# Routed-expert gate matrices built token by token from fp32r one-hots, one token behind each chunk of a projection unit

## What is computed

```python
q = (xb @ w_q).reshape(p, PEER_HEADS, 2, PEER_DK_HALF)
sc = jnp.einsum('phcd,hcnd->phcn', q, sub_keys)
top_s, top_i = lax.top_k(sc, PEER_TOPK)
...
best_s, best_pos = lax.top_k(cand_s, PEER_TOPK)
idx = jnp.take_along_axis(cand_i, best_pos, axis=-1)
g = jax.nn.softmax(best_s, axis=-1)
act = jax.nn.gelu(jnp.einsum('phkd,pd->phk', expert_u[idx], xb), approximate=False)
coef = g * act
return jnp.einsum('phk,phkd->pd', coef, expert_v[idx])
```

## Time and profile before

| | us |
|---|---|
| median of 3 runs (1960.28 to 1960.56) | 1960.36 |
| the profiled execution | 1959.54 |
| its span, first to last instruction | 1957.7 |
| mean granted clock, share of full | 0.965 |
| PE busy in the span | 1835.4 (94%) |
| DVE busy | 1579.7 (81%) |
| POOL busy | 1041.4 (53%) |
| ACT busy | 701.5 (36%) |

### The profile page before, as it was taken

One profiled execution on the slowest core, in us unless ns is written; L12 is line 12 of the kernel. 1 busy time (PEld: TensorE's weight loads), 2 busy tenths in 40 slices (PEclk: granted clock), 3 DMA queues, 4 the chain that ended last, 5 costly groups with the idle time before them and its releaser, 6 DMA issues.

```text
span 1957.7 us, 29019 instructions
## 1 busy us (share of the span) xinstructions
PE 1835.4 (94%) x10357; PEld 1593.5 (81%) x10357; DVE 1579.7 (81%) x2585; ACT 701.5 (36%) x1122; POOL 1041.4 (53%) x648
## 2 busy tenths in 40 slices
PE   8899889999999999999999999999999998988885
PEld 7677767999999899999978887888887676766664
DVE  6877777869898898888499999999997868757656
ACT  2333333433333444444433333333334333224441
POOL 1333235588888655555666676767774542344001
PEclk7898889999999999999999999999999998999988
DMA  7641242588999789899999999999995131200011
GB/s 297 222 167 54 65 162 84 181 303 308 314 310 316 249 295 309 300 307 306 320 351 358 354 354 351 354 352 353 364 353 175 55 96 54 76 22 3 2 59 50
DMA packets 159918, 440.49 MB, mean 225 GB/s; under 512 B 13648, under 2 KB 62928, under 8 KB 156752
## 3 DMA queue, kind: packets, MB, share of 16 engines
q1 hardware_dynamic: 64400, 254.71, 37.9%
q0 software_dynamic: 36864, 134.23, 18.2%
q10 hardware_dynamic: 58560, 50.34, 7.8%
HBM read 386.80 MB, written 52.43 MB: 224 GB/s over the span
## 4 chain that ended last, share of the span: by engine, by line
PE 71%; DVE 16%; issue 4%; POOL 4%; ACT 2%; DMA 2%; ACTq 0%; DVEq 0%; PEldq 0%; POOLq 0%
PE PS L947 32%; PE PS L1232 24%; PE PS L1195 4%; POOL w_lo L840 3%; DVE arena L2101 2%; PE PS L967 2%; ACT w_hi L1446 1%; DMA raw<-in_expert_v 1%; PE PS L1258 1%; DVE arena L1836 1%; PE PS L1267 1%; DMA arena<-in_expert_u_rows,arena 1%; POOL arena L888 1%; DVE arena L2128 1%; DVE arena L2125 1%
## 5 line engine op out<-in xcount | busy, mean ns | idle before, releaser
L840 POOL TENSOR_TENSOR w_lo<-raw,w_hi 128x1024 fp32r<-128x1024 f32 x299 | 719.2, 2406 | 786.1 <-ACT w_hi L1446 785.2
L1446 ACT ACTIVATE w_hi<-raw 128x1024 fp32r<-128x1024 f32 x332 | 351.7, 1060 | 982.8 <-PE PS L947 628.7
L947 PE MATMUL PS<-act_hi,w_hi 128*128 128x384 f32 (+1 forms) x1584 | 582.3, 368 | 25.3 <-POOL w_lo L840 19.0
L947 PE MATMUL PS<-act_hi,w_lo 128*128 128x384 f32 (+1 forms) x1584 | 567.4, 358 | 0.0
L947 PE MATMUL PS<-act_lo,w_hi 128*128 128x384 f32 (+1 forms) x1584 | 567.0, 358 | 0.0
L947 PEld LDWEIGHTS PS<-act_hi,w_hi 128*128 128x128 f32 x1584 | 302.2, 191 | 67.4 <-POOL w_lo L840 16.3
L947 PEld LDWEIGHTS PS<-act_hi,w_lo 128*128 128x128 f32 x1584 | 302.5, 191 | 22.8 <-issue 1.4
L947 PEld LDWEIGHTS PS<-act_lo,w_hi 128*128 128x128 f32 x1584 | 301.7, 190 | 23.6
L1232 PE MATMUL PS<-w_hi,act_hi 128*128 128x512 f32 x768 | 300.2, 391 | 7.0 <-ACT arena L1598 2.9
L1232 PE MATMUL PS<-w_lo,act_hi 128*128 128x512 f32 x768 | 299.3, 390 | 0.0
L1232 PE MATMUL PS<-w_hi,act_lo 128*128 128x512 f32 x768 | 299.2, 390 | 0.0
(11 more groups left out here) (347 smaller groups left out, 2001.5 us busy)
## 6 DMA issues: line engine op xcount, KB each, us to landing
raw<-in_expert_u SPq DMA_DIRECT2D x128, 512.0 KB, 5.3
raw<-in_expert_v SPq DMA_DIRECT2D x128, 512.0 KB, 6.0
raw<-in_w_in SPq DMA_DIRECT2D x52, 512.0 KB, 3.7
arena<-in_w_ada SPq DMA_DIRECT2D x24, 1024.0 KB, 7.2
gel_d<-arena ACTq DMA_DIRECT2D x64, 384.0 KB
gates_d<-arena ACTq DMA_DIRECT2D x12, 2048.0 KB, 15.9
arena<-gates_d SPq DMA_DIRECT2D x32, 768.0 KB, 7.0
arena<-gel_d SPq DMA_DIRECT2D x32, 768.0 KB, 9.1
```

Of the source, the lines that this page charges most:

```text
L840: pool.tensor_tensor(w_lo[:, k % SPLIT, :], raw[:, k % RAW, :], w_hi[:, k % SPLIT, :].bitcast(F32), ALU.subtract).then_inc(lo_split, 1)
L947: mm = pe.matmul(PS[:, bank, 0:n_tok], w[:, k % SPLIT, c * P:(c + 1) * P], x[:, c, 0:n_tok], start=(i == 0 and n == 0), stop=(i == KC - 1 ...
L1446: act.activation(w_hi[:, k % SPLIT, :], raw[:, k % RAW, :], ACT.Copy).then_inc(hi_split, 1)
```

## The change

One-hots are made for one token at a time by two DVE `tensor_scalar` operations of 128 elements, which read the numbers 0 to 127 from SBUF (`iota`) and write fp32r: `hot_row` (1 at i) and `hot_col` (the weight, rounded to fp32r, at j). A third operand, `hot_low`, is made on ACT: `hot_row` times the weight's low share. PE runs two fp32r matmuls per token, row by column and low by column, and they add up in PSUM. The operands lie in the free columns 384 to 511 of `act_hi` and `act_lo`, in a ring of five tokens. PE runs one token behind each of the eight chunks of a unit, and what is left over (a ninth token in some units) behind the unit; `unit_done` is now signalled with the last chunk's third product, ahead of that chunk's token. ACT makes the `hot_low`s in its list ahead of the `w_hi` of the next unit but one, and the gate copies and the stores stand between them. Five operations on 384 elements, one of them a reciprocal, prepare the low shares once on DVE. The copies to `routeT` are one where they were two. Semaphores are merged in places (`quad_in`, `c_tanh`, `c_ready`).

```diff
-ONEHOT = 16
+ONEHOT = 5
...
-        hot = region("hot", 8192, ONEHOT, 2, P)
+        hot_row = [act_hi[:, n, TD:T] for n in range(ONEHOT)]
+        hot_col = [act_lo[:, n, TD:T] for n in range(ONEHOT)]
+        hot_low = [act_hi[:, ONEHOT + n, TD:T] for n in range(3)] + [act_lo[:, ONEHOT + n, TD:T] for n in range(2)]
...
-        GATES_IN = [[g for g in range(TD // GROUP) if (N2 - N1 - 1) * g // (TD // GROUP) == k - 1] for k in range(N2 - N1)]
+        TOKENS_TO = [TD * k // (N2 - N1 - 1) for k in range(N2 - N1)]
...
+                    if i == KC - 1:
+                        mm.then_inc(unit_done, 1)
                     if between:
                         between(i, c)
-                mm.then_inc(unit_done, 1)
...
-            def gate_group(g):
-
-                if g >= 3:
+            def gate_token(n):
+
+                g, at, s_ = n // GROUP, n % GROUP, n % ONEHOT
+                if at == 0 and g >= 3:
                     pe.wait_ge(gate_sb, g - 2)
-                pe.wait_ge(hot_ready, g + 1)
-                for t in range(GROUP):
-                    n = (GROUP * g + t) % ONEHOT
-                    mm = pe.matmul(PS[:, 2 + g % 3, t * P:(t + 1) * P], hot[:, n, 0, :], hot[:, n, 1, :],
-                                   start=True, stop=True)
-                mm.then_inc(gate_ps, 1)
+                own = PS[:, 2 + g % 3, at * P:(at + 1) * P]
+                pe.wait_ge(hot_ready, 2 * n + 2)
+                pe.matmul(own, hot_row[s_], hot_col[s_], start=True, stop=False)
+                pe.wait_ge(low_ready, n + 1)
+                pe.matmul(own, hot_low[s_], hot_col[s_], start=False, stop=True).then_inc(gate_ps, 1)
...
+                def gates_between(i, _, first=first, last=last):
+                    if first + i < last:
+                        gate_token(first + i)
+
                 pe.wait_ge(gelu_done, u - 1)
-                linear(U_EU + u, u, u % 2, n_tok=TD)
+                linear(U_EU + u, u, u % 2, n_tok=TD, between=gates_between)
+                for n in range(first + KC, last):
+                    gate_token(n)
...
+            def low_token(n):
+
+                act.wait_ge(hot_ready, 2 * n + 1)
+                act.activation(hot_low[n % ONEHOT], hot_row[n % ONEHOT].bitcast(F32), ACT.Copy,
+                               scale=low_share[:, n:n + 1]).then_inc(low_ready, 1)
...
+                while lowered_to < min(TD, TOKENS_TO[k] + ONEHOT - 1 if k else 0):
+                    low_token(lowered_to)
+                    lowered_to += 1
+                    if GROUP * (groups_out + 1) + ONEHOT <= lowered_to:
+                        gates_out(groups_out)
+                        groups_out += 1
...
                 expert_act(u, u)
...
-            def one_hots(g):
-                if g >= 4:
-                    dve.wait_ge(gate_ps, g - 3)
-                at = slice(GROUP * g, GROUP * g + GROUP)
-                n = slice(GROUP * g % ONEHOT, GROUP * g % ONEHOT + GROUP)
-                chain.link(v.tensor_tensor(hot[:, n, :, :],
-                                           numbers.unsqueeze(1).unsqueeze(1).to_broadcast([P, GROUP, 2, P]),
-                                           routeT[:, 0:2, at].rearrange("p c t -> p t c").unsqueeze(3).to_broadcast(
-                                               [P, GROUP, 2, P]), ALU.is_equal))
-                v.tensor_tensor(hot[:, n, 1, :], hot[:, n, 1, :],
-                                weight_ps[:, at].unsqueeze(2).to_broadcast([P, GROUP, P]), ALU.mult).then_inc(hot_ready, 1)
+            def one_hots(n):
+
+                if n >= ONEHOT:
+                    dve.wait_ge(gate_ps, n - ONEHOT + 1)
+                v.tensor_scalar(hot_row[n % ONEHOT], iota[:, :], routeT[:, 0, n:n + 1], None, ALU.is_equal
+                                ).then_inc(hot_ready, 1)
+                v.tensor_scalar(hot_col[n % ONEHOT], iota[:, :], routeT[:, 1, n:n + 1], routeT[:, 2, n:n + 1],
+                                ALU.is_equal, ALU.mult).then_inc(hot_ready, 1)
...
-            dve.wait_ge(route_sb, 2 * GT)
+            dve.wait_ge(route_sb, GT)
             done = DOTS_A
+            w3 = routeT[:, 2, :].rearrange("p (a b) -> p a b", a=GT)
+            chain.link(v.tensor_copy(weight_hi, w3))
+            chain.post(v.tensor_tensor(low_share.rearrange("p (a b) -> p a b", a=GT), w3, weight_hi.bitcast(F32), ALU.subtract))
+            chain.link(v.tensor_scalar(low_div.rearrange("p (a b) -> p a b", a=GT), weight_hi.bitcast(F32), 1e-30, None, ALU.max))
+            chain.link(v.reciprocal(low_div, low_div))
+            chain.link(v.tensor_tensor(low_share, low_share, low_div, ALU.mult))
```

More of the change, by code:

```diff
@@ L1635, in gate_copy, with gates_out @@
                                PS[:, 2 + g % 3, :].rearrange("p (t j) -> p j t", t=GROUP), ACT.Copy).then_inc(gate_sb, 1)
+            def gates_out(g):
+                n, b = g // 8, g // 8 % 2
+                if g % 8 == 0 and n >= 2:
+                    act.wait_ge(gate_st[b], 16 * (n // 2))
+                gate_copy(g, b)
+                if g % 8 == 7:
+                    act.wait_ge(gate_sb, g + 1)
+                    act.dma_start(gates_d[:, :, n, :].rearrange("q p n -> p q n"),
+                                  stage_w[:, b, :].rearrange("p (q n) -> p q n", n=QUAD * WT)).then_inc(gate_st[b], 16)
@@ L1640, in _ @@
                 expert_act(u, u)
-                if u % 2:
+                if k == 0 and u % 2:
                     store_gel(u, u, u // QUAD)
-                for g in GATES_IN[k]:
-                    n, b = g // 8, g // 8 % 2
-                    if g % 8 == 0 and n >= 2:
-                        act.wait_ge(gate_st[b], 16 * (n // 2))
-                    gate_copy(g, b)
-                    if g % 8 == 7:
-                        act.wait_ge(gate_sb, g + 1)
-                        act.dma_start(gates_d[:, :, n, :].rearrange("q p n -> p q n"),
-                                      stage_w[:, b, :].rearrange("p (q n) -> p q n", n=QUAD * WT)).then_inc(gate_st[b], 16)
+            if (N2 - 1) % 2:
+                store_gel(N2 - 1, N2 - 1, (N2 - 1) // QUAD)
@@ L1653, in upper_coef @@
+            while groups_out < TD // GROUP:
+                gates_out(groups_out)
+                groups_out += 1
             def upper_coef(n, k, r=None):
```

47 lines of the change are left out of this document (24 added, 23 removed).

## The result

The changed kernel takes 2030.9 us (median of 4 runs, 2026.62 to 2033.41), the kernel before 1960.32 (1959.82 to 1960.56) beside it. The ratio is 1.0357, with a 95% interval of 1.034 to 1.0373: slower by 71 us. The profiled execution took 2026.62 us with a span of 2024.9. Forecast were 2019 us and a range of 1969 to 2070.

A forecast was written before the change was run, and what follows sets the result against it. PE bounds the kernel before; after the change DVE, stopped by POOL's `lower`, was to bound the stretch. 5.1 + 46 x 7.27 = 339.5 us against 280.3, +59 on 1959.5, gave 2019 us; range 1969 to 2070.

The forecast's parts named there:

- Exclusion of DVE by `lower`: Units 76 to 121: SBUF-only one-hots wait during POOL's 2.40 us `lower`, making DVE the bound at 7.27 us a unit.
- the signs that I named: In the stretch: 46 to 90 one-hots of 1 to 2.5 us, DVE busy nearly throughout, PE at 80 to 85%.
- What `lower` cost DVE: Per unit in the stretch: 2.40 us of `lower` less 0.15 hidden under a `row_dot` in progress.
- PE's price of a token: Two fp32r gate matmuls between chunks: 0.20 us a token, giving PE a floor of 5.92 us a unit.
- My bounds of 0.14 and 0.20: PE's two gate matmuls per token: 0.14 us if weight loads are hidden, 0.20 us if not.
- Stores "cost at nothing": ACT's list: `gel` and gate stores keep their number, only stand later, and were costed at nothing.
- The start: Start of the stretch: five DVE operations of 4.4 us, first token ready after 5.1 us, PE waiting some 4.
- the rival: Indirect DMAs in the stretch also stop DVE, 1.02 us a unit: 2066 us; chance 0.20, shared with poorer ring fit.
- the 1x mode: DVE's one-hots miss the faster mode and don't wait for POOL, but cost 0.065 us more each: 1965 us; chance 0.04.
- The faster case: Between chunks, two cheap fp32r matmuls at 0.14 us a token replace fp32 passes: -26 us, 1934 us; chance 0.09.
- PE waits for ACT's low share rather than for DVE: PE's waits in the stretch: sign that the sum counted the wrong engine; no size or chance given.

The follow-up runs named there:

- the fastest run: Kernel before with one fp32r product per token between chunks, one-hots in groups of four, ring of eight, gate stores on SP, no low share: 1939.7 us.

## Why the prediction was right

The direction, the main cause and, within 12 us, the time held: 2019 forecast, 2030.9 measured. By its steps:

- **Exclusion of DVE by `lower`.** Shown from both sides: away with one PSUM operand, away with a small `lower`. The period forecast was 7.27 us; the changed kernel has 7.29 (685.72 to 977.42 in 40 `w_hi`). The agreement is luck. DVE alone makes 7.08, as the run with SP stores shows, and the ACT issues, which the sum had at nothing, add 0.21. Of the signs that I named, 45 long operations were seen (46 to 90 forecast), DVE was busy 94% of the stretch, and PE 88% where I had 80 to 85.
- **What `lower` cost DVE.** In the changed kernel the two lines are busy 161.2 + 162.8 = 324.0 us in all. 384 times the two medians (0.275 + 0.335) are 234.2, so the stops cost 89.8 us, 1.95 us a unit. In the run with SP stores, where DVE hardly waits, they are busy 328.0 us, which makes 2.0 us a unit and leaves 5.1 of the 7.08 for DVE's own work, against my 5.02. For the stops I had put 2.40 - 0.15 = 2.25: more of a `lower` passes beside a `row_dot` than my 0.15.
- **PE's price of a token.** Put at 0.20 us, measured 0.223. My bounds of 0.14 and 0.20 did not hold it, nor did the 0.16 that I gave beside them: I took the load of the earlier trace rows for the full price of each matmul. Two together take more, one alone 0.12. I also added it to 4.25 us for the products, which holds the slower start of the products behind the gate matmuls; at 0.1735 us each the products take 4.16. Together that is 4.16 + 8.35 x 0.223 = 6.02 us a unit, what I had for the kernel before, and not 5.92. Since PE was not the bound, the sum did not feel it. In the kernels without exclusion and stores it decides.
- **Stores "cost at nothing".** This is the step that failed, and it is the 12 us. I looked at when the data is needed, not at what the issuing engine does meanwhile. The stores moved out of a list that PE ran ahead of into one that makes PE's next operand. The run with SP stores gives 13.9 us back. In the profiled executions its stretch takes 329.5 us (669.34 to 998.83) where the change takes 349.5, so the stores cost 20 us there: 9.7 are the stop at 982 us, behind the 40 `w_hi` of the period, and the rest is the 0.21 a unit. My 339.5 lies halfway, with DVE's pace 10 us too long and the stores 20 us too short. That the run with SP stores is so near my 2019 is luck too: what follows its stretch takes 1017 us where it took 1009 before, with PE waiting 8.77 us ahead of the second phase (before, 2.90 and 1.47), and I had counted no such thing.
- **The start.** 4 us of PE waiting were put down, 4.07 measured. The half clock behind it (products 0.32 us apart up to 675.6 us) was not counted. The kernel before has it here too, but only up to 672.4 us.
- **The rivals.** Indirect DMAs hardly stop the one-hots: twelve times for 0.16 us, 0.04 us a unit where the rival had 1.02, and in the run with PSUM numbers not at all (longest 0.423 us). L890's mean is 988 ns where it was 955. By the Trainium skill's box on DVE and SWDGE (SBUF — State Buffer) DVE's two-port operations keep GpSimd from writing descriptors; in the profile's records all that shows of it is these 33 ns. Nor is the 1x mode there: the median says so. The faster case fell with PE's price, though its mechanism is real for one product, as the fastest run shows. "PE waits for ACT's low share rather than for DVE" was my sign of a wrong sum. The waits show it (23 us against 13), and it is half true: 9.7 of the 23 us are the stop at 982, and without the low shares PE waits for DVE directly, in a kernel that is hardly faster. So most of the rest is DVE's delay passed on through ACT.

## What to carry to other kernels

Before an operation is moved from PSUM to SBUF operands for speed, look at what POOL does beside it: the shorter operation can be the one that is stopped, and its median will not tell, only its maximum. An engine that makes PE's next operand should not issue stores; look for issues of several us in its queue, even where they are hidden now, because work that ran ahead of them is what hides them. On an engine whose queue runs well ahead they may be as long and cost nothing. And a cheaper product that has to be done twice must be priced as a pair, between the neighbours it will have.
